# Gate and key rows, the shared key's rotation and the queries' rotation in other places of a gated-delta and latent-attention layer

## The reference, cut to what matters

```
proj = rmsnorm(x) @ w_in         -> gq gk gv gb ga gz | mq mkv mkr mz | lx lz
A: q, k = l2norm(silu(conv(gq, gk)));  v = silu(conv(gv))          (4 heads of 128)
   beta = sigmoid(gb);  g = -exp(a_log) * softplus(ga + dt)
   gated delta rule in chunks of 64 tokens: solve (I + tril(beta k k^T * decay)) X = I,
   u = X (v beta),  w = X (k beta exp(g));  then over 8 chunks, one after the other:
   v_new = u - w S;  o = (q exp(g)) S + attn v_new;  S = S exp(g_last) + (k exp(g_last-g))^T v_new
B: qm = rmsnorm(mq) @ w_uq  (8 heads: 128 plain + 64 rotated)
   kv = rmsnorm(mkv) @ w_ukv;  k_pe = rope(mkr), one key of 64 shared by all heads
   causal softmax attention with the joined plain and rotated parts
C: a gated linear recurrence on lx, lz
x + concat(A, B, C) @ w_out
```

## Time and profile before

| | |
|---|---|
| median of three runs | 2157.35 us |
| profiled execution | 2160.61 us, its span 2157.5 us |
| PE busy | 2045.2 us, 95% |
| DVE, ACT, POOL busy | 1260.0, 907.2, 646.8 us |
| mean granted TensorE clock | 0.97 |
| the touched stretch, layer 0 | 1160 to 1270 us of the span, then the scan to 1331 us |
| the touched stretch, layer 1 | 1720 to 1832 us, then the scan to 1893 us |

### The profile page before, as it was taken

How to read it: one execution, slowest core, us unless ns; L and a number is a source line. 1 busy time by engine, 2 the same in 40 slices (tenths; PEclk the granted TensorE clock), 3 DMA queues, 4 the chain that set the end, 5 groups by cost and what they waited for, 6 DMA issues and landing times. The chain is left out here.

```text
span 2157.5 us, 28176 instructions
## 1 busy us (share of the span) xinstructions
PE 2045.2 (95%) x10992; PEld 1546.7 (72%) x10992; DVE 1260.0 (58%) x1994; ACT 907.2 (42%) x1450; POOL 646.8 (30%) x308
## 2 busy tenths in 40 slices
PE   8999999999999999999999898999999988989997
PEld 6667874757668775667786777777877767867776
DVE  4688945547779854456658843535144877264332
ACT  4432255333432345333456444545234734254531
POOL 2323430223414431124443212223433431122252
PEclk9999999998999999999999999999999999989998
DMA  6223321142223231132322001112232210111232
GB/s 223 83 98 108 113 79 49 62 143 98 96 85 117 73 108 53 56 108 83 117 79 69 19 26 52 49 50 103 98 117 78 88 38 15 35 59 41 64 113 86
DMA packets 47858, 174.26 MB, mean 81 GB/s; under 512 B 5646, under 2 KB 6286, under 8 KB 46320
## 3 DMA queue, kind: packets, MB, share of 16 engines
q1 hardware_dynamic: 47600, 172.34, 23.5%
q10 hardware_dynamic: 128, 0.13, 0.0%
HBM read 157.77 MB, written 14.68 MB: 80 GB/s over the span
## 5 line engine op out<-in xcount | busy, mean ns | idle before, releaser
L2491 POOL TENSOR_TENSOR w_lo<-wraw,w_hi 128x1024 fp32r<-128x1024 f32 (+2 forms) x248 | 589.5, 2378 | 1358.1 <-ACT w_hi L1221 1358.1
L1221 ACT ACTIVATE w_hi<-wraw 128x1024 fp32r<-128x1024 f32 (+2 forms) x248 | 253.0, 1020 | 702.1 <-PE bank L623 413.7
L609 PE MATMUL bank<-h_hi,w_hi 128*128 128x512 f32 x1568 | 409.0, 403 | 1.1 <-ACT h_hi L1248 1.1
L618 PE MATMUL bank<-h_lo,w_hi 128*128 128x512 f32 x1568 | 388.7, 390 | 0.2
L623 PE MATMUL bank<-h_hi,w_lo 128*128 128x512 f32 x1536 | 379.5, 389 | 0.0
L609 PEld LDWEIGHTS bank<-h_hi,w_hi 128*128 128x128 f32 x1568 | 293.8, 191 | 92.7 <-issue 32.6
L618 PEld LDWEIGHTS bank<-h_lo,w_hi 128*128 128x128 f32 x1568 | 294.2, 188 | 64.0 <-DVE h_lo L1778 1.7
L623 PEld LDWEIGHTS bank<-h_hi,w_lo 128*128 128x128 f32 x1536 | 288.3, 188 | 59.9
L726 PE MATMUL bank<-arena,wdir 128*128 128x512 f32 x256 | 114.7, 599 | 1.1 <-DMA wdir<-in_w_direct 1.1
L1975 DVE CUSTOM_DVE_ANT_0 arena<-bank,arena 128x512 f32<-128x512 f32 x64 | 44.2, 691 | 89.7 <-PE bank L809 88.4
L726 PEld LDWEIGHTS bank<-arena,wdir 128*128 128x128 f32 x256 | 47.2, 190 | 66.3 <-issue 66.1
(11 more groups left out here) (403 smaller groups left out, 3267.0 us busy)
## 6 DMA issues: line engine op xcount, KB each, us to landing
wraw<-in_w_split SPq DMA_DIRECT2D x220, 512.0 KB, 3.2
wdir<-in_w_direct SPq DMA_DIRECT2D x16, 512.0 KB, 3.4
x_park<-arena SPq DMA_DIRECT2D x3, 2048.0 KB, 6.3
arena<-x_park SPq DMA_DIRECT2D x3, 2048.0 KB, 8.0
wraw<-in_w_split SPq DMA_DIRECT2D x12, 384.0 KB, 2.9
hg_park<-arena SPq DMA_DIRECT2D x2, 2048.0 KB, 8.7
arena<-hg_park SPq DMA_DIRECT2D x2, 2048.0 KB, 7.8
wraw<-in_w_split SPq DMA_DIRECT2D x16, 256.0 KB, 2.6
```

Source lines behind the costliest of these rows:

```text
L609: mm(ps[0:wd, 0:S], hi[:, k, :].bitcast(F32R), h_hi[:, k, :].bitcast(F32R), start=k == 0 and not begun, stop=False)
L618: ins = mm(ps[0:wd, 0:S], hi[:, k, :].bitcast(F32R), h_lo[:, k, :].bitcast(F32R), start=False, stop=bool(parts) and k == KT - 1)
L1221: a(w_hi[:, n % 2, 0:f].bitcast(F32R), wraw[:, n % 2, 0:f], ACT.Copy).then_inc(hi_done, 1)
L2491: nc.gpsimd.tensor_tensor(w_lo[:, n % 2, 0:f].bitcast(F32R), wraw[:, n % 2, 0:f], w_hi[:, n % 2, 0:f], ALU.subtract).then_inc(lo_done, 1)
```

## The change

ScalarE: `mq 1` is copied out right after `mq 0`, ahead of the four exponentials. The shared key's swap goes from behind the latent copies to level 4, ahead of the `qr` copy there. The `qr` tiles are copied out of their banks in levels 3 to 5 and after, and swapped from SBUF in the scan, behind chunks 1 to 4. `ckv_hi` waits for each normed latent key tile by itself.

VectorE: all four heads' beta products come first, then the four copies and `qg` products. The key's three rotation operations go from ahead of `kk` to the end of level 4. The queries' rotations go from levels 3 to 5 and after them into the scan, behind the state updates of chunks 2 to 5, and read SBUF alone.

```diff
+ROTATED_AT = (1, 2, 3, 4)
...
                 keep(("mq", l, 0), cq[:, 0, :])
+                keep(("mq", l, 1), cq[:, 1, :])
                 for tt in range(NT):
                     act.wait_ge(*after("dclip", l, tt))
                     a(dtm[:, tt, :, :], dtm[:, tt, :, :], ACT.Exp).then_inc(up("dexp", l, tt), 1)
-                keep(("mq", l, 1), cq[:, 1, :])
...
-                swap_halves(kr, tmp[:, 0, :], "kr_rot", l)
...
                 def turn_queries(h):
-                    await_split("qr", l, h)
                     act.wait_ge(*((after("kr", l), after("ckv_norm", l, 1))[h] if h < 2 else after("qr_sb", l, h - 2)))
-                    swap_halves(bank("qr", l, h), tmp[:, h % 2, :], "qr_rot", l, h)
+                    swap_halves(qr[:, h, :], tmp[:, h % 2, :], "qr_rot", l, h)
...
+                    if n == 4:
+                        swap_halves(kr, tmp[:, 0, :], "kr_rot", l)
...
                     if n >= 3:
-                        turn_queries(n - 3)
+                        keep(("qr", l, n - 3), qr[:, n - 3, :])
                     if n == 4:
                         for j in range(2):
+                            act.wait_ge(*after("ckv_norm", l, j))
                             a(ckv_hi[:, j, :].bitcast(F32R), ckv[:, j, :], ACT.Copy).then_inc(up("ckv_hi", l, j), 1)
-                turn_queries(3)
+                keep(("qr", l, 3), qr[:, 3, :])
...
+                    if ck in ROTATED_AT:
+                        turn_queries(ROTATED_AT.index(ck))
...
                     dve.wait_ge(*read("gB", l, h, 0))
+                for h in range(H):
                     dve.wait_ge(*after("egb", l, h))
                     link(v.tensor_copy(egl[:, h, :], qg[:, h, CH - 1:S:CH]))
                     v.tensor_tensor(qg[:, h, :], qg[:, h, :], qB[:, h, :], ALU.mult).then_inc(up("qg", l, h), 1)
                     dve.wait_ge(*after("qg", l, h))
 
-                dve.wait_ge(*after("kr_rot", l))
-                link(v.tensor_tensor(kr[:, :], kr[:, :], cosT, ALU.mult))
-                link(v.tensor_tensor(tmp[:, 0, :], tmp[:, 0, :], sinT, ALU.mult))
-                v.tensor_tensor(kr[:, :], kr[:, :], tmp[:, 0, :], ALU.add).then_inc(up("kr", l), 1)
-                dve.wait_ge(*after("kr", l))
...
                 def rotate(h):
 
                     dve.wait_ge(*after("qr_rot", l, h))
-                    v.tensor_tensor(qr[:, h, :], bank("qr", l, h)[:, 0:S], cosT, ALU.mult).then_inc(release("qr", l, h), 1)
                     link(v.tensor_tensor(tmp[:, h % 2, :], tmp[:, h % 2, :], sinT, ALU.mult))
-                    dve.wait_ge(*read("qr", l, h))
+                    link(v.tensor_tensor(qr[:, h, :], qr[:, h, :], cosT, ALU.mult))
                     v.tensor_tensor(qr[:, h, :], qr[:, h, :], tmp[:, h % 2, :], ALU.add).then_inc(up("qr_sb", l, h), 1)
...
-                        if n >= 3 and tt == 1:
-                            rotate(n - 3)
...
+                        rotate_keys()
...
-                rotate(3)
-
...
+                    if ck - 1 in ROTATED_AT:
+                        rotate(ROTATED_AT.index(ck - 1))
```

More of the change, by code:

```diff
@@ L2291, in _, with rotate_keys @@
                 dve.wait_ge(*read("qk", l, NT - 1))
+                def rotate_keys():
+                    dve.wait_ge(*after("kr_rot", l))
+                    link(v.tensor_tensor(kr[:, :], kr[:, :], cosT, ALU.mult))
+                    link(v.tensor_tensor(tmp[:, 0, :], tmp[:, 0, :], sinT, ALU.mult))
+                    v.tensor_tensor(kr[:, :], kr[:, :], tmp[:, 0, :], ALU.add).then_inc(up("kr", l), 1)
+                    dve.wait_ge(*after("kr", l))
                 def rotate(h):
                     dve.wait_ge(*after("qr_rot", l, h))
-                    v.tensor_tensor(qr[:, h, :], bank("qr", l, h)[:, 0:S], cosT, ALU.mult).then_inc(release("qr", l, h), 1)
                     link(v.tensor_tensor(tmp[:, h % 2, :], tmp[:, h % 2, :], sinT, ALU.mult))
-                    dve.wait_ge(*read("qr", l, h))
+                    link(v.tensor_tensor(qr[:, h, :], qr[:, h, :], cosT, ALU.mult))
                     v.tensor_tensor(qr[:, h, :], qr[:, h, :], tmp[:, h % 2, :], ALU.add).then_inc(up("qr_sb", l, h), 1)
```

## The result

The changed kernel takes 2136.45 us, the median of four runs (2135.83 to 2138.09), beside 2157.22 for the kernel before on the same chip (2153.92 to 2158.64). The ratio is 0.9893 [0.9872, 0.9915]: 20.8 us faster, where I forecast 2133. The time lies inside the range and inside the forecast's own range. The profiled execution took 2135.83 us, its span 2133.8, which is 23.7 us shorter than the span of before.

The account below looks back on a forecast made before the run. TensorE, busy nearly the whole span, was taken as the bound: its work plus waits and half clock. Gains of 1.0 + 7.0 + 16.0 = 24.0 us took the median from 2157.35 to 2133 us; range 2124 to 2144.

Parts of the forecast that it names:

- Part 1: Gate rows: early `mq 1` copy starts `mq 2` 1.0 us sooner, 0.5 lost to slow clock; 1.0 us in both layers.
- my upper end of 2.4: Gate rows: `mq 2` up to 2.4 us sooner per layer if the clips are not blocked by GpSimd.
- Part 2: Around the column sums: key rotation out of the `kk` stage, beta products first; idle time and half clock go, 7.0 us.
- The 0.6 us that I took off for ScalarE's root: Column sums: deduction of 0.6 us for ScalarE's second root, which the slow time had hidden.
- Part 3: Levels 3 to 5, `qr 0` to the scan: query rotations moved out, waits and half clock go; 16.0 us.
- the 31.7 to 32.5 that I had named: Sign of being right: 31.7 to 32.5 us from `qr 0` to the scan.
- The 7.85 and 8.75 us of the prediction: Levels 3 to 5: what the undisturbed length of 31.7 us saves against 39.55 and 40.43 us in the two layers.
- rival B: Level 4: key's work becomes the wait, GpSimd covers the second norm, clock falls; 9.4 us lost, 2143 us; chance 0.18.
- Part 4: The scan: ScalarE's added copies and VectorE's rotations fit within the slack of `su`; cost 0.
- A: Gate rows: clips pass GpSimd and clock holds, up to 3.9 us per layer, 7 more in all, 2126; chance 0.14.
- C: The scan: rotations wait for late ScalarE swaps, delaying the chunks; 8 us slower, 2165; chance 0.04.
- The last link of its chain: The scan: a late subtraction delays `su`, the state update and next chunk, each microsecond costing TensorE one in 8 chunks.

Follow-up runs that it names:

- the first part alone: The kernel before with only `mq 1` copied out ahead of the four exponentials: 2154.81 us, ratio 0.9983.
- the queries alone: The kernel before with only early `qr` copies, swaps and rotations in the scan, and the `ckv_hi` waits; key work stays ahead of `kk`: 2149.27 us, ratio 0.9959.

## Why the prediction came out as it did

**Part 1, right in mechanism and size.** Forecast 1.0 us sooner per layer and 0.5 lost to the clock; measured 1.14 and 1.13 sooner, with 0.13 and 0.52 lost. The clips wait for GpSimd, 2.01 us instead of 0.90, which I had read off a blocked copy. The page "SBUF — State Buffer" of the Trainium skill, section "Who interferes with whom", names the operations of both, `tensor_scalar` and `copy`, among those that can contend with GpSimd, and the clips' row agrees. The experiment with the split put later shows what it costs: another 1.1 us, so that `mq 2` begins 2.25 us sooner per layer, near my upper end of 2.4.

**Part 2, right but for one term.** 8.4 us against 7.0. The two idle times (3.0 each, 2.92 and 2.93 forecast) and layer 1's 1.70 us of half clock are gone. After that gap one of the two layers paid 1.4 to 1.7 us of half clock in each of the four kernels that kept it, and the other layer 0.65 between `X0` and `qr 0`. The 0.6 us that I took off for ScalarE's root has no counterpart: `X0` to `qr 0` is unchanged in layer 1 and 0.66 us shorter in layer 0, where the kernel before still had half clock. The term should have been nothing. VectorE's second `kk` operation was blocked (1.93 us from 1193.89), as I had foreseen, and `X0` did not wait for it. The split loop over heads is worth nothing, as costed.

**Part 3, the length after right, the gain in part luck.** 15.7 us against 16.0; 32.12 and 32.18 us inside the 31.7 to 32.5 that I had named. That end point is solid: the clock is full there. The starting point is not. The kernel with the first part alone took 38.33 us for the old levels, and from there the gain is 12.4 us; the other 3.3 are half clock that its trace did not have. The 7.85 and 8.75 us of the prediction took this half clock as a fixed loss, on one trace.

The reason was incomplete too. The prediction counts the key's swap in level 4 as a cost that fits, and what I expected of the queries alone was the whole gain; alone they leave 33.71. The last 1.6 us per layer need the swap in front of the split, which holds GpSimd's piece back until the second norm is almost done. My rival B had the two times in hand: by its count the norms end 0.1 us before GpSimd starts, and in the trace they end 0.04 after, with the second norm already running. What I did not ask is where the piece would lie without the swap: over the norms, as before. The kernel with the swap behind the copy shows the harm of B, at 1.6 us per layer where B had 4.7: the clock stayed at 1.00.

**Part 4, right.** The scan's length is the same to 0.01 us. VectorE's idle time before the subtraction is gone, the rotations do not wait for the swaps, and the subtraction comes before TensorE needs it.

**The rivals.** A, the fuller gain, did not come: the clips are blocked. With the clips freed it is worth 1.1 us per layer more, of which slow clock takes 0.6 back, where I had counted 3.4: the half clock that I had put into it did not go. C did not come either. The last link of its chain is real: with six more products the subtraction comes late, `su` waits, and the kernel is slower than before. Its first link, a rotation that waits for a late swap, no run tested.

**From 25.7 to 20.8.** The prediction subtracted 24.0 from both the profiled execution and the median. The stretches gave 25.7; 1.9 were lost in parts that the change does not touch; 1.1 were gained outside the span (3.1 us of the execution before, 2.0 after); and the profiled execution of before lay 3.4 us above its median, that of the changed kernel 0.6 below: 25.7 - 1.9 + 1.1 - 3.4 - 0.6 = 20.9. The 24.0 of the forecast is thus 1.7 us less than the stretches gave and 3.2 more than the medians show. The time of one kernel moves by such amounts with where half-clock pieces fall: over this study single executions of the kernel before ran from 2149.94 to 2168.05 us. The 3.3 us of half clock in the old levels 3 to 5 are of the size of the 3.4 by which that execution lay above its median. That the one is the other is not shown; the step is inferred from the clocks of such stretches, and no run isolated it.

## What to carry to other kernels

When work is moved on an engine, follow what it delays on the engine behind it: here a swap of ScalarE in front of a weight split kept GpSimd off VectorE's norms, worth 1.6 us per layer, and the same swap one step later lost it. Move work into a loop only up to the slack of its slowest return path, counted with GpSimd beside it; two extra products per rotated chunk cost 1.05 us per layer, six cost 15. Compare small changes by the starts of the same product in both traces: medians of kernels a few microseconds apart hid what the stretches showed to a tenth. But trust the tenth only where the granted clock is 1.00 in both traces. A stretch with half clock in it, such as the old levels 3 to 5, differed by 1 to 2 us between two traces of the same instructions, and needs more than one.

## What the runs showed of the hardware

- VectorE's `SCALAR_TENSOR_TENSOR` on two SBUF operands is held up by GpSimd: two norms took 1.54 us when GpSimd's 1.8 us piece started in the last 0.04 of them, and 3.04 to 3.07 when it started 0.7 us into them. The same operation with one operand in a bank took 4.87 us for eight, with and without GpSimd.
- The blocking goes both ways: GpSimd's 128x512 piece took 1.74 us beside back-to-back products of VectorE and 1.29 in other chunks of the same scan (1.27 to 1.29).
- A long gap of TensorE costs about as much again in half clock, and not each time: 6.9 us of waits in four gaps, the longest 3.8, lengthened the scan by 15.0 us, at a granted clock of 0.89. After the gap of 2.92 us before the column sums the ten products took 4.56 us in one layer and 6.26 in the other. Short waits (0.55 and three of 0.23, 1.24 us, instead of a single 0.23) lengthened their stretch by 1.5 to 1.6 at a clock of 1.00.
- Levels 3 to 5 with the same instructions and the same waits on the query rotation took 39.55 us at a clock of 0.91 in one trace and 38.33 at 0.96 in another.
